# Softmax normalisation in three attentions: from GpSimd to VectorE, GpSimd keeps one mask

## The reference, cut to what matters

```
first block:   s = q k^T * 64^-0.5 + t5_bias;  causal mask;  p = softmax(s);  out = p v      (8 heads)
second block:  s = q k^T * scale + rpb bias (window mask);   p = softmax(s);  out = p v      (16 heads)
MLA layer:     s = (q_nope k_nope + q_rope k_rope) * scale;  p = softmax(s);  out = p v      (16 heads)
```

## Time and profile before

| What | Time |
|---|---|
| median of 3 runs | 1284.73 us (1284.29 to 1289.89) |
| the profiled execution | 1287.22 us |
| its span in the trace | 1285.1 us |
| TensorE busy | 1236.4 us (96%) |
| VectorE busy | 1030.0 us (80%) |
| ScalarE busy | 788.2 us (61%) |
| GpSimd busy | 89.5 us (7%) |

### The profile page before, as it was taken

One profiled execution on the slowest core, in us unless ns is written; L12 is line 12 of the kernel. 1 busy time (PEld: TensorE's weight loads), 2 busy tenths in 40 slices (PEclk: granted clock), 3 DMA queues, 4 the chain that ended last, 5 costly groups with the idle time before them and its releaser, 6 DMA issues.

```text
span 1285.1 us, 20248 instructions
## 1 busy us (share of the span) xinstructions
PE 1236.4 (96%) x7622; PEld 1097.9 (85%) x7622; DVE 1030.0 (80%) x1108; ACT 788.2 (61%) x1010; POOL 89.5 (7%) x111
## 2 busy tenths in 40 slices
PE   6989999999999999999999989999999999999995
PEld 5978999987898799998897758888989898989884
DVE  6887899896755577777856578888898989898987
ACT  5774666544555554434346656777777777777764
POOL 0020000000562100000002202000000000000020
PEclk9999999999999999999999999999999999999998
DMA  9963997679934569987983228999999999999992
GB/s 314 340 227 99 313 325 268 229 292 257 260 107 163 191 207 323 326 303 293 392 265 109 75 86 330 405 387 361 393 353 401 360 393 346 409 347 408 340 410 83
DMA packets 163835, 369.04 MB, mean 287 GB/s; under 512 B 24404, under 2 KB 96415, under 8 KB 157367
## 3 DMA queue, kind: packets, MB, share of 16 engines
q1 hardware_dynamic: 157201, 350.73, 76.3%
q10 hardware_dynamic: 5094, 12.11, 2.5%
q0 software_dynamic: 1472, 5.28, 1.1%
HBM read 360.72 MB, written 14.70 MB: 292 GB/s over the span
## 4 chain that ended last, share of the span: by engine, by line
PE 79%; DVE 11%; ACT 4%; issue 4%; DMA 1%; ACTq 0%; POOL 0%; DVEq 0%; SPq 0%
PE ps L1316 22%; PE ps L776 8%; PE ps L778 8%; PE ps L777 8%; PE ps L1343 6%; PE ps L789 5%; PE ps L791 5%; PE ps L793 5%; DVE wlo L1910 3%; PE ps L859 2%; PE ps L851 2%; DVE alo L1910 1%; DVE wlo L1903 1%; PE ps L988 1%; PE ps L974 1%
## 5 line engine op out<-in xcount | busy, mean ns | idle before, releaser
L1379 ACT ACTIVATE whi<-raw 128x1024 fp32r<-128x1024 f32 x190 | 197.0, 1057 | 165.1 <-PE ps L778 112.2
L1903 DVE TENSOR_TENSOR wlo<-raw,whi 128x1024 fp32r<-128x1024 f32 x190 | 232.6, 1250 | 80.8 <-ACT whi L1379 77.8
L776 PE MATMUL ps<-ahi,whi 128*128 128x256 f32 x864 | 247.1, 286 | 2.7 <-DVE alo L1935 2.5
L778 PE MATMUL ps<-ahi,wlo 128*128 128x256 f32 x864 | 245.2, 284 | 0.0
L777 PE MATMUL ps<-alo,whi 128*128 128x256 f32 x864 | 245.2, 284 | 0.0
L1910 DVE TENSOR_TENSOR wlo<-raw,whi 128x1792 fp32r<-128x1792 f32 (+1 forms) x96 | 199.3, 2089 | 26.5 <-ACT whi L1392 25.4
L1392 ACT ACTIVATE whi<-raw 128x1792 fp32r<-128x1792 f32 (+1 forms) x96 | 166.9, 1755 | 57.9 <-PE ps L1316 29.1
L776 PEld LDWEIGHTS ps<-ahi,whi 128*128 128x128 f32 x864 | 166.5, 193 | 4.2 <-issue 3.8
L777 PEld LDWEIGHTS ps<-alo,whi 128*128 128x128 f32 x864 | 166.5, 193 | 0.7 <-issue 0.7
L778 PEld LDWEIGHTS ps<-ahi,wlo 128*128 128x128 f32 x864 | 166.5, 193 | 0.0
L1316 PE MATMUL ps<-whi,hchi 128*128 128x448 f32 x352 | 102.9, 374 | 5.6 <-DVE hclo L2464 3.3
(11 more groups left out here) (356 smaller groups left out, 2417.0 us busy)
## 6 DMA issues: line engine op xcount, KB each, us to landing
raw<-in_moe_w_gu SPq DMA_DIRECT2D x96, 896.0 KB, 6.7
ada<-in_w_ada SPq DMA_DIRECT2D x48, 1024.0 KB, 7.2
raw<-in_moe_w_down SPq DMA_DIRECT2D x32, 1024.0 KB, 7.9
ada<-in_moe_w_gu SPq DMA_DIRECT2D x32, 896.0 KB, 7.5
raw<-in_w_up SPq DMA_DIRECT2D x22, 1024.0 KB, 6.1
raw<-in_ffn_w_gu SPq DMA_DIRECT2D x22, 1024.0 KB, 8.8
ada<-in_moe_w_down SPq DMA_DIRECT2D x16, 1024.0 KB, 9.0
raw<-in_na_w_qkv SPq DMA_DIRECT2D x12, 1024.0 KB, 7.6
```

Of the source, the lines that this page charges most:

```text
L776: pe.matmul(o, h[:, k, cols], bhi[:, k], start=(k == 0), stop=False)
L778: m = pe.matmul(o, l[:, k, cols], bhi[:, k], start=False, stop=(k == KT - 1))
L1379: act.activation(high_, src, ACT.Copy).then_inc(hi_done, 1)
L1903: ve.tensor_tensor(low_, src, high_.bitcast(F32), ALU.subtract).then_inc(lo_done, 1)
```

## The change

VectorE's `reciprocal_sums` now multiplies the probabilities itself: the reciprocal is linked (`own.link` raises VectorE's own semaphore and waits for it), then come the two products, the second of which raises `a_norm`. The semaphore `a_rsum` and GpSimd's `attention` are gone. GpSimd's list then begins with both masks.

```
             def reciprocal_sums(n, h):
                 ve.wait_ge(sem("a_exp"), HEADS0[n] + h + 1)
-                ve.reciprocal(rsum[:, h, :], sume[:, h, :]).then_inc(sem("a_rsum"), 1)
+                own.link(ve.reciprocal(rsum[:, h, :], sume[:, h, :]))
+                for qt, col, w in attention_plan(n)[2]:
+                    v = core[n][1][:, h % 4, col:col + w]
+                    m = ve.tensor_scalar(v, v, rsum[:, h, qt:qt + 1], None, ALU.mult)
+                m.then_inc(sem("a_norm"), 1)

         @block.gpsimd
         def _(po):
-            def attention(n, heads):
-                seg = attention_plan(n)[2]
-                for h in heads:
-                    po.wait_ge(sem("a_rsum"), HEADS0[n] + h + 1)
-                    for qt, col, w in seg:
-                        v = core[n][1][:, h % core[n][1].shape[1], col:col + w]
-                        m = po.tensor_scalar(v, v, rsum[:, h, qt:qt + 1], 1.0, ALU.mult, ALU.mult)
-                    m.then_inc(sem("a_norm"), 1)
...
-            attention(1, range(H1))
             mask_bias2(0)
-            attention(2, range(4))
             mask_bias2(1)
-            attention(2, range(4, H2))
             po.wait_ge(mm_done, 2 * W_MDN)
             po.dma_start(rope, a["consts"][:, C_ALL:C_ALL + R_ALL]).then_inc(sem("rope_in"), 16)
-            attention(3, range(H2))
```

## The result

| | before | after |
|---|---|---|
| median, measured together (8 runs each) | 1284.55 us | 1292.07 us |
| ratio after to before | | 1.0050, 95% interval 1.0039 to 1.0061 |
| median, measured together once more later (32 and 9 runs) | 1285.25 us | 1290.46 us |
| ratio after to before | | 1.0041, 95% interval 1.0028 to 1.0054 |
| the profiled execution; its span | 1287.22; 1285.1 us | 1292.16; 1289.9 us |

The changed kernel is slower by 5 to 7.5 us. The forecast was +3.9 us and 1288.6 us, so the direction was right and the amount was short: the first median lies above the forecast's own range of 1286.5 to 1290.5 and the second just inside it. Two lines of the page of the changed kernel: busy time by engine, and the chain that ended last.

The account below looks back on a forecast made before the run. TensorE was taken as the bound (79% of the chain of waits), so only its idle time around the attentions counts: 1.9 + 0.35 + 1.65 + 0 = +3.9 us on 1284.73 gives 1288.6 us; own range 1286.5 to 1290.5, whole range 1281.5 to 1293.

Parts of the forecast that it names:

- the rival with the early mask: Second attention: early mask holds VectorE's products and splits, TensorE stops, clock drops; 1293.9 us, chance 0.12.
- the second mask at a cost of nothing: Second attention: mask runs about 339 to 352, splits end at 351.5, TensorE covered until about 353.3; cost 0.
- the stop at 336: Second attention: TensorE's idle 2.33 us at 336.10 in the profile before, followed by 1.2 GHz; given no term.
- First attention: 60 to 103 us: `outputs_lo` before the output projection comes later, +1.9 us, ends +1.2 to +2.4.
- The price of a head: On VectorE, each head's two products add 0.58 us in the first attention, 0.65 with two 128x256.
- The list of four products ahead of `outputs_lo`: First attention: odd heads of steps 0 to 2 and step 3's even head delay `outputs_lo`, 4 x 0.58 = 2.3 us.
- Second attention, steps 6 and 7: `outputs_lo` 0.65 later, sums wait 0.6, 0.25 wait of transposes goes; +0.35 us, between 0 and +0.6.
- Third attention: 686 to 729 us: later `outputs_lo` makes the next step's sums wait; +1.65 us, ends +0.6 to +2.4.
- The +1.0 of step 5: Third attention: sums already waited 0.33, so 0.65 counts in full, plus first reciprocal of step 4 about 0.3 late.
- The four steps with a gate sum: Third attention: 0.45 us slack against a shift of 0.65 leaves 0.2 new wait each, +0.7 us together.
- the cover: Rival: products fit VectorE's idle time and the waits for GpSimd were the price; 1282.3 us, chance 0.25.
- the 1.47 us wait before the output projection: Rival, first attention: TensorE idles 1.2 to 1.7 us there and its clock could drop; 1290.1 us, chance 0.13.

Follow-up runs that it names:

- it alone: Only the first attention's products moved to VectorE, the rest as in the kernel before: 1286.81 us against 1285.74, ratio 1.0011 (1.0000 to 1.0023).
- the second attention alone: Kernel before with only the second attention's products on VectorE, both masks directly behind each other: 1287.96 us against 1285.57, ratio 1.0024.
- the third alone: Kernel before with only the third attention's products on VectorE: 1285.96 us against 1285.74, ratio 1.0004 (0.9994 to 1.0014).
- both masks placed: Changed kernel with the first mask behind the first four `wlo` splits, the second behind the fourth head's products: 1287.29 us, ratio to before 1.0022.
- the combined one: Kernel before with second and third attention on VectorE, even head's products behind `outputs_lo` from the third step, both masks held later: ratios 0.9990 and 0.9982.
- the kernel with products behind `outputs_lo`: Changed kernel with the even head's products behind `outputs_lo` from the third step on: 1287.68 us, ratio to before 1.0024 (1.0013 to 1.0036).

## Why the prediction was short

The place of the loss was forecast, its amount was not. 1292.07 us lies in the whole range of 1281.5 to 1293, but that range reached so far only for the rival with the early mask, whose 1293.9 is nearer to the first measurement than the forecast's 1288.6. Two steps failed: the second mask at a cost of nothing, and the stop at 336, which the sum left out as if it stood in both kernels alike.

**First attention: right.** +1.9 predicted, +1.78 in the trace, +1.4 us (0 to 3) in time for it alone by its ratio. The price of a head was right as well, 0.57 and 0.64 for 0.58 and 0.65 (the recorded terms add up to 0.59 and 0.67). The list of four products ahead of `outputs_lo`, the useless gain of the GpSimd waits, and the scan's return to 0.69 us were as argued.

**Second attention, steps 6 and 7: right.** The sums wait 0.64 (0.6 predicted) and the 0.25 for GpSimd is gone. Its going gave back 0.47 in the shift of the matmuls, so the sum is +0.18 where +0.35 was taken.

**Third attention: mechanism right, one term too large.** +1.65 predicted, +1.15 found (1.31 in the table, of which 0.2 is the second attention's end). The +1.0 of step 5 measured +0.74. The four steps with a gate sum each got their new wait, as forecast: the shift of the sums against before grows by 0.15, 0.21, 0.21 and 0.27 (at 700.07, 704.90, 714.17 and 718.99 of before), together 0.84 where 0.7 and 0.25 were taken. The sums at 704.90 for instance come at 707.77 now, 0.15 behind the end of `outputs_lo` (707.20 + 0.42). The wait for GpSimd gave back 0.37 instead of 0.26, and 0.08 more went behind step 5.

**The second mask: failed.** "Cover about 2 us; cost 0" took the 2.2 us per split but let the products through at full speed, although the rival below it had the products held for a mask instruction each. The products took 2.15 and 2.47 us a pair. This cost 0.7 us in the profiled execution and waits of 0.38 and 1.28 in the second. I was wrong, by the condition I gave, in the latter: an idle time of more than 1 us between 345 and 370. The rival with the early mask was right in the mechanism. Its price of 5.3 us was too high for the changed kernel, whose pairs were held about 1.7 us each, not 3.7. In the profile of the second attention alone, where TensorE had no earlier stop and the weights came late as well, the loss was 4.6 us (103.44 against 98.84 with the third alone, whose weights were as late).

**The baseline: the assumption nobody had priced.** The 2.33 us stop at 336 was read as a constant that stands in both kernels. It is a race. SP's list of small transfers sets when the first table lands and the mask starts, 324.7 to 327.8 in the nine profiles where nothing holds it, with the same mean (326.6 and 326.7) whether the first attention is on GpSimd or on VectorE. VectorE's `alo` products start at 325.2 to 326.2 with it on GpSimd and at 326.5 to 327.1 with it on VectorE. So the first attention's lateness moves them into the mask. The stop was in one of four profiles of the first kind and in five of five of the second, one of these with 0.57 us. Such counts suggest it and do not prove it; what is shown is that in no profile with the first mask held did TensorE stop there. With both masks placed the ratio is 1.0022, by an interval that overlaps the changed kernel's second one.

**The sum.** Products +2.75 us where no mask stops TensorE; the rest of the 5.2 to 7.5 goes with the masks' place, as far as the profiles show. How the rest divides between more frequent stops at 336 and the early second mask is open: the medians of 8 to 12 runs that spread over 5 us do not separate them. (The ends of the recorded sum, +1.8 to +5.4, give 1286.5 to 1290.1, not 1290.5, and the third attention's terms add up to 1.69.)

The two other rivals fell: the cover did not hold (1282.3), and the 1.47 us wait before the output projection left the clock at 2.4 GHz.

## What to carry to other kernels

Before a stop in the profile is taken as fixed, ask whether a load's landing decides it, and look at a second execution: here one race was worth 3.4 us, almost as much as the whole forecast. Work moved to a nearly full engine costs where something waited for is queued behind it, so put it behind that. And freeing an engine lets what is left on it start earlier: say where, and hold it there if that place is bad.

## What the hardware showed that I had not expected

- Beside GpSimd's mask, VectorE's `alo` products with two SBUF inputs took 1.6 to 1.7 us instead of 0.63 (6.42 to 6.80 and 2.50 for four), splits 2.24 instead of 1.2, pairs of products with one SBUF input up to 2.47 in the changed kernel and once 4.13 (in the combined one, beside the first mask) instead of 0.62, while a reduction of 128x512 kept its 0.69 us and the scores from PSUM their 0.68. The Trainium skill (SBUF — State Buffer, "Who interferes with whom") says this of the kinds: VectorE's instructions with two SBUF inputs, and the likes of these products when they run in a two-port mode, share a port pair with GpSimd under an exclusive lock, and reductions never do. The rows agree.
- GpSimd's mask of eight pieces took 14.3 to 15.75 us beside the splits, 10.05 to 10.18 when held behind them.
- An idle time of 1.90 us of TensorE was followed by 0.63 and 0.52 of the full clock in the next two stretches of 2 us (2.4 and 1.2 GHz mixed), one of 1.67 us by 1.00. In one execution (the kernel with products behind `outputs_lo`) the granted clock read 0.95 everywhere from 330 to 342, and no half clock followed a 2.30 us stop.
- The router's stretch took 20.2 us in most profiles and 21.5 to 21.8 in four, where TensorE's clock fell to 1.2 GHz without a longer wait of TensorE before it: a second source of scatter. The four are among the eight profiles with the first attention on GpSimd; of the six with it on VectorE none shows it. Whether that is chance is open.
